# Which expert's weights are loaded and split ahead of the expert loop

## What is computed

```python
def grouped_moe(u, w_router, router_bias, w_gate, w_up, w_down):
    scores = softmax(t @ w_router)
    sel = scores + router_bias          # top-1 of 4 groups by the sum of its two best,
    ...                                 # then the two best experts of that group
    hg = einsum('td,edf->tef', t, w_gate)
    hu = einsum('td,edf->tef', t, w_up)
    h = silu(hg) * hu * combine[..., None]
    y = einsum('tef,efd->td', h, w_down)

h = h + g2 * grouped_moe(rmsnorm(h, norm2_g) * (1 + sc2) + sh2, ...)
```

## Time and profile before

| what | value |
|---|---|
| median of the runs | 1855.15 us |
| the profiled execution's own time | 1855.65 us |
| span of its trace, first to last instruction | 1853.9 us |
| PE busy | 1560.0 us, 84% |
| DVE busy | 1222.1 us, 66% |
| ACT busy | 784.2 us, 42% |
| POOL busy | 739.3 us, 40% |
| HBM read / written | 276.55 MB / 36.81 MB |
| chain that ended last | PE 64%, DMA 13%, DVE 12%, ACT 5%, issue 4% |

### The profile page before, as it was taken

The page is one execution under the profiler, slowest core; times in us unless marked ns, Lnnn a source line. Parts: engine busy times, 40 slices in busy tenths (PEclk is TensorE's granted clock), DMA queues, the critical chain, the costliest instruction groups (busy, mean ns, idle before and its releaser), DMA issues.

```text
span 1853.9 us, 23253 instructions
## 1 busy us (share of the span) xinstructions
PE 1560.0 (84%) x8890; PEld 1340.4 (72%) x8890; DVE 1222.1 (66%) x1660; ACT 784.2 (42%) x1178; POOL 739.3 (40%) x427
## 2 busy tenths in 40 slices
PE   2699899989999884999649989988999988399980
PEld 0589766679999673777438986677999967377760
DVE  0559488878955454778194947887885445477735
ACT  0413477762224132776142246786222413166721
POOL 2113399521112201799312329872111220179840
PEclk7799899999999885999869999999999988599995
DMA  7612155412222634899862215501232262479964
GB/s 292 196 52 69 32 204 185 145 36 80 81 69 69 250 112 159 313 367 368 304 218 74 63 36 182 171 1 35 69 85 65 80 249 83 180 267 363 372 243 182
DMA packets 128814, 296.54 MB, mean 160 GB/s; under 512 B 11224, under 2 KB 80984, under 8 KB 108912
## 3 DMA queue, kind: packets, MB, share of 16 engines
q1 hardware_dynamic: 102944, 216.02, 34.1%
q10 hardware_dynamic: 10560, 40.90, 5.8%
q0 software_dynamic: 15200, 38.14, 5.7%
HBM read 276.55 MB, written 36.81 MB: 169 GB/s over the span
## 4 chain that ended last, share of the span: by engine, by line
PE 64%; DMA 13%; DVE 12%; ACT 5%; issue 4%; POOL 1%; POOLq 0%; DVEq 0%; ACTq 0%; SPq 0%
PE ps L552 27%; PE ps L511 9%; PE ps L813 6%; DMA raw<-in_w_down 3%; PE ps L620 3%; PE ps L610 3%; DVE gu_lo L1518 2%; PE ps L859 2%; DMA raw<-in_w_up 2%; PE ps L457 2%; PE ps L599 2%; PE ps L879 2%; DMA raw_x<-in_w_down 2%; DMA raw<-in_w_ada 1%; PE ps L600 1%
## 5 line engine op out<-in xcount | busy, mean ns | idle before, releaser
L2304 POOL TENSOR_TENSOR w_lo<-raw,w_hi 128x1024 fp32r<-128x1024 f32 (+1 forms) x46 | 162.5, 3534 | 557.5 <-ACT w_hi L1123 557.5
L552 PE MATMUL ps<-u_hi,w_hi 128*128 128x320 f32 x768 | 239.9, 312 | 5.3 <-ACT probs L1222 5.3
L552 PE MATMUL ps<-u_lo,w_hi 128*128 128x320 f32 x768 | 239.0, 311 | 0.0
L552 PE MATMUL ps<-u_hi,w_lo 128*128 128x320 f32 x768 | 238.9, 311 | 0.0
L1123 ACT ACTIVATE w_hi<-raw 128x2048 fp32r<-128x2048 f32 (+1 forms) x64 | 101.3, 1591 | 289.6 <-PE ps L552 134.8
L1876 DVE SCALAR_TENSOR_TENSOR glu<-glu,convw 128x670 f32<-128x670 f32 x164 | 170.9, 1042 | 5.5
L552 PEld LDWEIGHTS ps<-u_hi,w_hi 128*128 128x128 f32 x768 | 145.4, 189 | 5.9 <-ACT probs L1222 5.8
L2412 POOL DMA_INDIRECT xe<-u_d,tab_u x34 | 78.0, 2294 | 178.2 <-issue 143.7
L552 PEld LDWEIGHTS ps<-u_lo,w_hi 128*128 128x128 f32 x768 | 145.6, 190 | 0.1
L552 PEld LDWEIGHTS ps<-u_hi,w_lo 128*128 128x128 f32 x768 | 145.4, 189 | 0.0
L1733 DVE TENSOR_TENSOR pt_lo<-ps,pt_hi 128x512 fp32r<-128x512 f32 x160 | 109.6, 686 | 24.9 <-ACT pt_hi L1248 22.0
(11 more groups left out here) (379 smaller groups left out, 4239.1 us busy)
## 6 DMA issues: line engine op xcount, KB each, us to landing
raw<-in_w_ada SPq DMA_DIRECT2D x44, 1024.0 KB, 5.1
raw<-in_w_in SPq DMA_DIRECT2D x48, 512.0 KB, 5.1
raw_x<-in_w_gate SPq DMA_DIRECT2D x16, 1024.0 KB, 6.8
raw<-in_w_up SPq DMA_DIRECT2D x16, 1024.0 KB, 8.1
raw_x<-in_w_down SPq DMA_DIRECT2D x16, 1024.0 KB, 9.1
raw_x<-in_w_up SPq DMA_DIRECT2D x14, 1024.0 KB, 8.3
raw<-in_w_gate SPq DMA_DIRECT2D x14, 1024.0 KB, 6.1
raw<-in_w_down SPq DMA_DIRECT2D x14, 1024.0 KB, 9.1
```

The costliest lines, as they stand in the source:

```text
L552: ins = mm(ps[:, b, 0:HALF], (w_hi, w_lo)[w][:, s, cols(k):cols(k) + P], xs[x][:, k, half * HALF:(half + 1) * HALF], start=(k == 0 and w + ...
L2304: g_.tensor_tensor(w_lo[:, n % 2, 0:k], raw[:, n % 2, 0:k], w_hi[:, n % 2, 0:k].bitcast(F32), ALU.subtract).then_inc(*G.up("g_lo", "w_lo", n))
```

## The change

The order of units begins with expert 2's gate and up: (2,0) (2,1) (1,0) (1,1) (1,2), and from (3,0) on it is as before. `e0_gu` moves to the bytes of `w_hi` (`R_W`), which the last projection has finished with; the overflow loop keeps the old place under a name of its own, `over_gu`. ACT makes the high halves of (2,0), (2,1) and (1,2) during the routing, DVE the low half of (2,0) there, and POOL the low halves of (2,1) and (1,2). In step 0 of the expert loop these six instructions are gone. The rows of experts are gathered by the same indirect DMAs as before.

```diff
-GATE_UP_DOWN = [(1, 0), (1, 1)]
-for e in range(NE - 1):
+GATE_UP_DOWN = [(2, 0), (2, 1), (1, 0), (1, 1), (1, 2)]
+for e in range(1, NE - 1):
     GATE_UP_DOWN += [(e + 2, 0), (e + 2, 1)] if e + 2 < NE else []
     GATE_UP_DOWN += [(e + 1, 2)]
...
-    e0_gu = at("e0_gu", [P, 2, KC, DE], F32, R_A + 8 * KB)
+    e0_gu = at("e0_gu", [P, 2, KC, DE], F32, R_W)
+    over_gu = at("over_gu", [P, 2, KC, DE], F32, R_A + 8 * KB)
...
@@ ScalarE, behind the output projection
             spread(NT - 1)
+            eng.wait_ge(*A.at("filled", ("wo", 1, NT - 1)))
+            hi_expert(UNIT_OF[2, 0])
             ha_tr(NT - 1, 1)
             eng.dma_start(ha_d.rearrange("(t p) d -> p t d", p=P), h_a[:, :, :]).then_inc(*A.up("ha_out", "ha_out", by=16))
             eng.wait_ge(*A.at("u2", NT - 1))
             eng.dma_start(u2_d.rearrange("(t p) d -> p t d", p=P), u2[:, :, :]).then_inc(*A.up("u2_st", "u2_out", by=16))
+            hi_expert(UNIT_OF[2, 1])
...
             act(xe[:, :, :], ident[:, 0:1].unsqueeze(2).broadcast_to([P, 2, D]), ACT.Copy, scale=0.0).then_inc(*A.up("a_xe", "xe_zero"))
+            eng.wait_ge(*A.at("filled", ("router",)))
+            hi_expert(UNIT_OF[1, 2])
             eng.wait_ge(*A.at("u2_out"))
             hi_expert(UNIT_OF[1, 0])
             hi_expert(UNIT_OF[1, 1])
...
@@ ScalarE, the expert loop
                 xt_hi_of(e + 1)
-                if e + 2 < NE:
+                if 0 < e < NE - 2:
                     hi_expert(UNIT_OF[e + 2, 0])
...
-                if e + 2 < NE:
+                if 0 < e < NE - 2:
                     hi_expert(UNIT_OF[e + 2, 1])
-                if e + 1 < NE:
-                    if e:
-                        eng.wait_ge(*A.at("y_full", e - 1))
+                if 0 < e < NE - 1:
+                    eng.wait_ge(*A.at("y_full", e - 1))
                     hi_expert(UNIT_OF[e + 1, 2])
...
@@ VectorE
             u2_of(NT - 1)
 
+            lo(UNIT_OF[2, 0])
             eng.wait_ge(*V.at("filled", ("router",)))
...
-                if e + 2 < NE:
+                if 0 < e < NE - 2:
                     lo(UNIT_OF[e + 2, 0])
                     lo(UNIT_OF[e + 2, 1])
...
@@ GpSimd
             for n in range(U_CO, U_MOE):
                 lo(n)
 
+            lo(UNIT_OF[2, 1])
+            lo(UNIT_OF[1, 2])
             eng.wait_ge(*G.at("tab"))
...
-                if e + 1 < NE:
+                if 0 < e < NE - 1:
                     lo(UNIT_OF[e + 1, 2])
```

More of the change, by code:

```diff
@@ L874, in down, with gate_up_f @@
                 return ins
-            def gate_up_f():
+            def gate_up_f(gu):
                 for x in range(2):
                     for k in range(KC):
-                        ins = mm(ps[:, 2, x * DE:(x + 1) * DE], xt_f[:, k, :], e0_gu[:, x, k, :], start=(k == 0), stop=(k == KC - 1))
+                        ins = mm(ps[:, 2, x * DE:(x + 1) * DE], xt_f[:, k, :], gu[:, x, k, :], start=(k == 0), stop=(k == KC - 1))
                 return ins
@@ L905, in _ @@
                     eng.wait_ge(*T.at("e0_in", 1))
-                    gate_up_f().then_inc(*T.up("gu_full", "gu_full", e))
+                    gate_up_f(e0_gu).then_inc(*T.up("gu_full", "gu_full", e))
                 else:
@@ L928, in _ @@
                 eng.wait_ge(sems("ov_raw1"), 16 * o)
-                gate_up_f().then_inc(sems("ov_gu"), 1)
+                gate_up_f(over_gu).then_inc(sems("ov_gu"), 1)
                 eng.wait_ge(sems("ov_h"), o)
@@ L1042, in unit, with whole @@
                 load(n, (r(n, (KC, KC, 2)[k]), io[part(k)][l, e, :, :].rearrange("(p c) n -> p c n", p=P)))
-            def first_expert(k):
-                return e0_dn[:, :, :] if k == 2 else e0_gu[:, k, :, :]
+            def whole(gu, k):
+                return e0_dn[:, :, :] if k == 2 else gu[:, k, :, :]
             for e, k in GATE_UP_DOWN[0:4]:
@@ L1051, in _ @@
             for k in range(2):
-                eng.dma_start(first_expert(k), io[part(k)][l, 0, :, :].rearrange("(p c) n -> p c n", p=P)).then_inc(*S.up(f"e0_raw{k}", "e0_in", k, by=16))
+                eng.dma_start(whole(e0_gu, k), io[part(k)][l, 0, :, :].rearrange("(p c) n -> p c n", p=P)).then_inc(*S.up(f"e0_raw{k}", "e0_in", k, by=16))
             eng.wait_ge(*S.at("u2", NT - 1))
             eng.sem_inc(sems("passed_S"), 1)
-            eng.dma_start(first_expert(2), io[part(2)][l, 0, :, :].rearrange("(p c) n -> p c n", p=P)).then_inc(*S.up("e0_raw2", "e0_in", 2, by=16))
+            eng.dma_start(whole(e0_gu, 2), io[part(2)][l, 0, :, :].rearrange("(p c) n -> p c n", p=P)).then_inc(*S.up("e0_raw2", "e0_in", 2, by=16))
             for e, k in GATE_UP_DOWN[4:]:
@@ L1070, in over @@
                     src = io[part(k)][l, bass.ds(of, 1), :, :].rearrange("a (p c) n -> p (a c) n", p=P)
-                    eng.dma_start(first_expert(k), src).then_inc(sems(f"ov_raw{k}"), 16)
+                    eng.dma_start(whole(over_gu, k), src).then_inc(sems(f"ov_raw{k}"), 16)
                 eng.wait_ge(sems("ov_gu"), o)
```

## The result

The changed kernel takes 1866.77 us in the median of 7 runs (1863.89 to 1872.86), against 1854.36 us of the kernel before (7 runs beside it, 1848.29 to 1857.06). The ratio is 1.0065, with a 95% interval of 1.005 to 1.008. By this ratio the change makes the kernel 12.1 us slower (9 to 15). The profiled execution is the longest of the seven, 1872.86 us, with a span of 1871.1 us.

What follows compares the result with a forecast made beforehand. Loop: DMA and PE both near full; ahead of it, DVE's uncovered chain of small instructions sets the start. Terms 2.4 + 2.8 + 8.6 - 0.6 = 13.2 us gave 1868.4 us, range 1856 to 1874 us.

Steps and rivals of the forecast that it cites:

- High halves on ACT and low half of (2,0) on DVE, nothing: Routing: ACT's and DVE's added instructions fit idle time or hold up nothing, so they cost 0 us.
- First hold: Routing: POOL's low half of (2,1) makes DVE's L1974 wait, 2.4 us in the first layer and 2.8 in the second.
- Second hold: Routing: POOL's low half of (1,2) holds DVE's chain of small instructions, 4.3 us a layer, 8.6 us in all.
- Head start: Expert loop: earlier weight loads gain only 0.3 us a layer, 0.6 us in all, since (4,1) is issued no earlier.
- the bound of 6.5 us a layer: Expert loop: most a head start could bring, 0.43 us a step over 15 steps, with PE's step taken as 9.71 us.
- Step 0 loses nothing: First loop step: removing the six instructions gains nothing, since PE waited for nothing behind them.
- the second hold did not miss the chain: Routing rival: (1,2) lands so late that POOL starts behind 715.7 us; only 4.6 us remain, 1859.8 us; chance 0.12.
- the loop did not fall to PE's step: Expert loop rival: holds as forecast, but loop runs at PE's step, +0.8 us, 1856.0 us; chance 0.08.
- the faster side: Rival: small instructions escape POOL's holds and the loop runs at 9.71 us a step, -13.0 us, 1842.1 us; chance 0.08.
- an unchanged time: Rival for the whole kernel: neither a hold nor a gain, 1855 us; chance 0.03.
- what would have made it slower than forecast: Rival: lower PE clock lengthens expert 0's product or a gather meets more loads, about 1871 us and up; chance 0.05.

Runs made afterwards that it cites:

- the second group: The changed kernel run once more with no edit, against the kernel before: 1862.17 us, ratio 1.0055.
- The run with only this hold: Changed kernel with the low half of (2,1) moved to DVE behind the table, only that of (1,2) left on POOL in the routing: 1855.93 us, ratio 1.0013.
- the two kernels with late halves: Changed kernel with low halves of (2,1) and (1,2) made later: on POOL behind the second gather, 1850.99 us; on DVE behind expert 1's, 1850.79 us.
- those with five: Fifth weight buffer added to the kernel with late halves on DVE, 1835.39 us, or to the kernel before with loads behind the first gather, 1840.12 us.
- the one with six: Sixth weight buffer added to the changed-order kernel with five buffers and late halves on DVE: 1834.68 us, ratio 0.9878 to the kernel before.

## Why the prediction was right

The forecast was 1868.4 us, +13.2; measured +12.1 and, in the second group, +10.2 (6 to 14). By its steps:

- **High halves on ACT and low half of (2,0) on DVE, nothing:** right. The table load ended at 695.50 us, well before the exponential at 698.90, and DVE still waited for the logits.
- **First hold, 2.4 + 2.8 = 5.2 us:** 3.16 - 0.24 and 2.64 - 0.24 give 2.9 and 2.4 us, together 5.3. The mechanism is right. That the sum fits to 0.1 us is luck: by layers it was 0.5 us too low and 0.4 too high, and in the second execution the two were 2.4 and 2.5.
- **Second hold, 8.6 us:** the mechanism is right, the size is the term that was off. The routing grew by 5.63 + 5.45 = 11.1 us, so 5.8 us are left for it, 2.9 a layer. The holds themselves were 3.96 and 4.00 us, not 4.3; that is 0.6 of the 2.8 us. The larger part is that I didn't ask whether the chain had a wait of its own behind the held instruction. It had one, 0.97 us for PE, twice. The run with only this hold shows 4.3 us a layer where that wait lies ahead of it. So the sentence that whatever delays one of the small instructions moves the whole loop by the same amount was wrong at this place. Nor do nearly all instructions of the chain have both inputs in SBUF: in the stretch from 704.1 to 713.3 us of the kernel before it is 24 of 38, which is still enough for one to be met soon (it came 0.4 us behind POOL's start).
- **Head start, -0.3 us a layer:** right in kind. (4,1) went out 17.10 us behind the first `sg` in both kernels. In the changed one the DMA engines stood nearly idle in the first 20 us of the loop (share 0.16, before 0.56), and no loop gain can be told from the scatter. But the bound of 6.5 us a layer was too low: with PE's step at 9.37 us the loads cost 11 us a layer. I had taken the shortest step in sight for PE's own; the third step of the changed kernel, 9.38 us, shows PE's own.
- **Step 0 loses nothing:** right; its first two steps are 9.0 and 10.0 us in all kernels.
- **Not foreseen:** the loads beside the first gather. They lengthen it by some 1.6 to 1.9 us in the kernel before and in the changed one, so it changed nothing in the difference, but removing it is what made the two kernels with late halves faster than before.

The sum thus is 11.1 us instead of 13.2: one term 2.8 us too large, one 0.6 us gain not seen. The measured 1866.77 us lies inside the range of 1856 to 1874. The rivals: the second hold did not miss the chain (POOL began it at 707.43 us, the table's product at 720.93); the loop did not fall to PE's step; the faster side needed holds under 2 us a layer, and they were 5.5; an unchanged time is excluded by the interval; and of what would have made it slower than forecast nothing came, since the stretch from table to first `sg`, gather and expert 0's product included, was 0.5 us shorter over both layers.

## What to carry to other kernels

An idle engine isn't free to use if it shares something with the one on the critical path: before moving work to GpSimd, look what VectorE does at that time, and price the hold as the rest of GpSimd's instruction less any wait that the chain has next. A transfer made earlier gains nothing when the next one still waits for the same buffer: look for the first load whose release did not move. Where the DMA engines are full in a loop and idle in its first steps, another buffer is the edit to try (here it took 11 us or 0.6% out of the two loops), and it also closed some gaps in the steady state.

## What the runs showed of the hardware

- A subtraction of 128x2048 on GpSimd held VectorE instructions with two inputs in SBUF, of 128x10 to 128x80 elements, for its whole rest (up to 4.43 us for 0.17), and a copy with a single input of 2 elements a partition as well (4.45 us). A reduction, a reciprocal and an instruction with one input in PSUM passed. A fill on GpSimd held nothing.
- The first indirect gather of 128 rows took 5.1 to 5.4 us with no weight load beside it and 7.0 to 7.2 us with two or three loads of 1 MB issued while it ran.
- In the 110 us from 20 us into the loop on, both layers taken, the kernels with four buffers and full loads moved 359 to 370 GB/s at a DMA share of 0.96 to 0.98, those with five 375 to 382 and the one with six 381 to 383, at 0.98 to 0.99. From five to six the rate hardly rose; there the gain is the load moved into the idle 20 us.
